# Inverting the delta rule's triangular matrices on 64x64 blocks, two products side by side in the array

## The chip, the cores and the metric

The kernel runs on one core of one Trainium2 chip. The metric is the device time of one execution in microseconds (us). Several engines work beside each other on their own instruction queues: TensorE (PE; its weight loads are listed apart as PEld), VectorE (DVE), ScalarE (ACT), GpSimd (POOL) and SyncE (SP), which issues most transfers. They meet through semaphores.

## The reference

The reference is a two-layer hybrid block (attention, state-space scan, stick-breaking attention, feed-forward nets), followed by a second block. In the second block a gated delta net (8 heads of width 64, 256 tokens) stands beside a window attention, and a mixture of experts comes after it. All inputs are float32. What matters here is the delta rule, which the reference computes in chunks of 64 tokens:

```
m = jnp.where(strict, jnp.einsum('bhncd,bhnsd->bhncs', kb, k) * decay, 0.0)
eye = jnp.eye(CHUNK, dtype=jnp.float32)
a_mat = eye + m
t_mat = lax.linalg.triangular_solve(a_mat, jnp.broadcast_to(eye, a_mat.shape),
                                    left_side=True, lower=True)
u = jnp.einsum('bhncs,bhnse->bhnce', t_mat, vb)
w = jnp.einsum('bhncs,bhnsd->bhncd', t_mat, kb * jnp.exp(G)[..., None])
attn = jnp.einsum('bhncd,bhnsd->bhncs', q, k) * decay
```

The output of a delta rule does not depend on the length of the chunks; the kernel takes chunks of 128 tokens, so that it has two chunks (t = 0, 1) of 8 heads: 16 triangular matrices of 128x128 to invert.

## The kernel before, in words

Nearly all of the kernel is matrix products with weights that stream through a ring of buffers; each is split in a rounded part and a rest (`round_chunk` L247 on ACT, `split_chunk` L251 on DVE) and multiplied in three passes (`three`, L264 to L266). The change is in one class, `DeltaRule`, which runs once, between the input projection of the second block (`Project`) and `WindowAttention`. During it SP and POOL have nothing to do; the next weights already lie in the ring.

Heads are handled in two groups, e = 0 and e = 1 (even and odd heads); a group has 8 matrices, s = 4t + h. Three engines work in an order written out by hand, and every engine takes its instructions in program order:

- `pe_spread` (L2195) writes the cumulated decay of each head along a row, `dve` subtracts the column's own (L2401), ACT takes the exponential (L2312), and DVE multiplies by the causal mask (L2406). `pe_gram` (L2203) makes k^T kb and k^T q with 64 rows of the array for each product: e = 0 lies in rows 0 to 63, e = 1 in rows 64 to 127. DVE multiplies them with the decays to `mT` (L2409) and `aT` (L2414).
- Then the inverse T of I + M grows by doubling. At level v the inverses of the diagonal blocks of size 2^v are known, and `LmT` holds the part of M that couples neighbouring blocks (`mT` times the mask of the level, L2411 and L2421). PE makes L T (`l_times_t`, L2220), ACT and DVE copy it out of PSUM (L2318 and L2418), PE makes T L T and its transpose (`update`, L2227 and L2228), and DVE subtracts both (L2436 and L2437) and masks the next `LmT`. There are 7 levels for 128 rows: the first needs no update product, the last only one; levels 2 to 6 run in a hardware loop (`Fori`). Each product is 128x128x128 and takes two records of PE. Both T and its transpose `Tt` are kept, since a product needs its stationary operand transposed.
- The tail (L2252 to L2274) uses `Tt` for the values of the first chunk, the state, and the second chunk; ACT brings the output to `br` (L2325), and DVE normalises it (L2462).

Of the kernel before, what the change touches and what calls it, by code (L numbers as in the profile page):

```python
# [34 lines left out]
P = 128  # L35
# [31 lines left out]
LEVELS = 7  # L67
# [20 lines left out]
def shape_constants():  # L88
# [11 lines left out]
    ]  # L100
    for b in [1 << n for n in range(LEVELS)]:
        parts.append((f"level{b}", ((j // b) % 2 == 1) & (p // b == j // b - 1)))
# [29 lines left out]
def build(nc, A, out, stop=99):  # L132
# [1957 lines left out]
    class DeltaRule:  # L2090
# [13 lines left out]
        SPREAD_BANK, KK_BANK, QK_BANK, FIRST_BANK = (0, 6), (2, 4), (0, 6), (2, 4)  # L2104
        level, lt, upd = sem("g_level"), sem("g_lt"), sem("g_upd")
        lt0_done, lt1_done = sem("g_lt0_done"), sem("g_lt1_done")
        u0, u0_done, wT_done, state, state_done = (sem(f"g_{n}") for n in ("u0", "u0_done", "wT_done", "state", "state_done"))
        vnew, vnew_done, out_done = sem("g_vnew"), sem("g_vnew_done"), sem("g_out")
# [11 lines left out]
        LT = e  # L2120
        LmT = [view(room, 12288 + 1024 * e, 8, P) for e in range(2)]
        T = [merged[:, e, :].rearrange("p (s n) -> p s n", n=P) for e in range(2)]
        Tt = [view(xT_work, D * e, 8, P) for e in range(2)]
        vn = [view(hi_ring, 3072 + 512 * e, 8, HD2) for e in range(2)]
# [25 lines left out]
        def pool(self, pool):  # L2150
# [8 lines left out]
            self.multiply(nc.gpsimd, self.kd, self.k_, self.tab[:, 5, 0, :], 0).then_inc(self.scaled2, 1)  # L2159
            pool.wait_ge(pow_asked, power(2))  # L2160
# [45 lines left out]
        def pe(self, pe):  # L2206
# [7 lines left out]
            heads = self.heads  # L2214
            carry(pe)

            def l_times_t(e, stat, bank=None):
                for t, h in heads:
                    s = 4 * t + h
                    ins = pe.matmul(ps[:, (4 * e if bank is None else bank) + t, h * P:(h + 1) * P], self.LmT[e][:, s, :], stat(s), start=True, stop=True)  # L2220
                ins.then_inc(self.lt, 1)

            def update(e, both):
                for t, h in heads:
                    s, cols = 4 * t + h, slice(h * P, (h + 1) * P)
                    if both:
                        pe.matmul(ps[:, 4 * e + 2 + t, cols], self.Tt[e][:, s, :], self.LT[e][:, s, :], start=True, stop=True)  # L2227
                    ins = pe.matmul(ps[:, 4 * e + t, cols], self.LT[e][:, s, :], self.Tt[e][:, s, :], start=True, stop=True)  # L2228
                ins.then_inc(self.upd, 1)
            for e in range(2):  # L2230
                pe.wait_ge(self.level, e + 1)
                l_times_t(e, lambda s: ident, self.FIRST_BANK[e])
            with pe.Fori(0, LEVELS - 2) as v:
                for e in range(2):
                    pe.wait_ge(self.level, v * 2 + (e + 3))
                    l_times_t(e, lambda s: self.T[e][:, s, :])
                for e in range(2):
                    pe.wait_ge(self.lt0_done, v * 2 + (e + 1))
                    pe.wait_ge(self.lt1_done, v * 2 + (e + 1))
                    update(e, True)  # L2240
            for e in range(2):
                pe.wait_ge(self.level, LEVELS * 2 + e - 1)
                l_times_t(e, lambda s: self.T[e][:, s, :])
            for e in range(2):
                pe.wait_ge(self.lt0_done, LEVELS * 2 + e - 3)
                pe.wait_ge(self.lt1_done, LEVELS * 2 + e - 3)
                update(e, False)
            cols = lambda h: slice(h * HD2, (h + 1) * HD2)
            for e in range(2):
                pe.wait_ge(self.level, LEVELS * 2 + e + 1)  # L2250
# [3 lines left out]
                ins.then_inc(self.u0, 1)  # L2254
            for e in range(2):
                pe.wait_ge(self.u0_done, e + 1)
                for h in range(4):
                    ins = pe.matmul(ps[:, 4 * e + 2, cols(h)], self.both(self.kd, 0, h), self.vn[e][:, h, :], start=True, stop=True)
                ins.then_inc(self.state, 1)
            for e in range(2):  # L2260
                pe.wait_ge(self.wT_done, e + 1)
                pe.wait_ge(self.state_done, e + 1)
# [4 lines left out]
                ins.then_inc(self.vnew, 1)  # L2267
            for e in range(2):
                pe.wait_ge(self.vnew_done, e + 1)
# [5 lines left out]
                ins.then_inc(self.out_done, 1)  # L2275
# [29 lines left out]
        def act(self, act):  # L2305
# [9 lines left out]
            with act.Fori(0, LEVELS - 1) as v:  # L2315
                for e in range(2):
                    act.wait_ge(self.lt, v * 2 + (e + 3))
                    nc.scalar.copy(self.LT[e][:, 0:4, :], view_bank(4 * e, 4, P)).then_inc(self.lt0_done, 1)  # L2318
            for e in range(2):
                act.wait_ge(self.u0, e + 1)  # L2320
                nc.scalar.copy(self.rows(self.wT, e), self.rows(view_bank(4 * e + 1, 4, P), e)).then_inc(self.wT_done, 1)
            for e in range(2):
                act.wait_ge(self.out_done, e + 1)
# [63 lines left out]
        def dve(self, dve):  # L2387
# [7 lines left out]
            lev = consts[:, CONSTS["level1"][0]:CONSTS["level1"][0] + LEVELS * P].rearrange("p (v n) -> p v n", n=P)  # L2395
            dve.wait_ge(self.scaled2, 1)
            for e in range(2):
                dve.wait_ge(self.gram, (self.SPREAD0, self.SPREAD1)[e])
                for s in range(8):
                    t, h = divmod(s, 4)  # L2400
                    ins = V.tensor_scalar(self.e[e][:, s, :], ps[:, self.SPREAD_BANK[e] + t, h * P:(h + 1) * P], self.tab[:, 1, t, 2 * h + e:2 * h + e + 1],  # L2401
                                          0.0, ALU.subtract, ALU.min)
                ins.then_inc(self.seg, 1)
            for e in range(2):
                dve.wait_ge(self.dec, e + 1)
                V.tensor_tensor(self.e[e], self.e[e], bc(const("upto").unsqueeze(1), [P, 8, P]), ALU.mult)  # L2406
                dve.drain()
                dve.wait_ge(self.gram, self.KK)
                V.tensor_tensor(self.mT[e], self.e[e], big(self.KK_BANK[e]), ALU.mult)  # L2409
                dve.drain()  # L2410
                V.tensor_tensor(self.LmT[e], self.mT[e], bc(lev[:, 0:1, :], [P, 8, P]), ALU.mult).then_inc(self.level, 1)  # L2411
            dve.wait_ge(self.gram, self.QK)
            for e in range(2):
                V.tensor_tensor(self.aT[e], self.e[e], big(self.QK_BANK[e]), ALU.mult)  # L2414
            eye = bc(ident.unsqueeze(1), [P, 8, P])

            def copy_lt(e):
                V.tensor_copy(self.LT[e][:, 4:8, :], view_bank(4 * e + 1, 4, P)).then_inc(self.lt1_done, 1)  # L2418

            def next_level(e, mask):  # L2420
                V.tensor_tensor(self.LmT[e], self.mT[e], bc(mask, [P, 8, P]), ALU.mult)  # L2421
                dve.drain()
                dve.sem_inc(self.level, 1)
            for e in range(2):
                dve.wait_ge(self.lt, e + 1)
# [1011 lines left out]
```

## Time and profile before

| | |
|---|---|
| Median of 3 runs | 2549.4 us (2544.87 to 2549.5) |
| Profiled execution | 2549.39 us, of which the span 2547.5 us |
| PE busy | 2315.7 us, 91% of the span |
| DVE busy | 1683.0 us, 66% |
| ACT busy | 1157.6 us, 45% |
| Mean granted clock of TensorE | 0.939 of full speed |
| Delta rule, from the end of L2401 to the first product of the tail | 1938.74 to 2027.75 us of the span |
| Its tail | 2027.75 to 2062 us |

"Busy" is the share of time in which the engine has an instruction under way. The granted clock is 1.0 at 2.4 GHz and 0.5 at 1.2 GHz. Line numbers (L2220) are those of the kernel before.

### The profile page before, as it was taken

How to read it: one execution, taken by the hardware profiler on the slowest of the kernel's cores; microseconds unless marked ns; L12 is line 12 of the kernel's file. 1: busy time of each engine (PE TensorE's matmuls, PEld its weight loads, DVE VectorE, ACT ScalarE, POOL GpSimd, SP SyncE). 2: the span in 40 equal slices, each digit the busy share in tenths (PEclk: the TensorE clock that was granted, in tenths of full speed). 3: DMA queues.
4: the chain of work that ended last, by engine and by line, in shares of the span. 5: the costliest groups of instructions: out<-in, count | busy, mean ns of one | idle time of the engine just before them, and what ended most of it. 6: DMA issues, size and time to landing. Idle time of an engine off the chain costs nothing.

```text
span 2547.5 us, 32468 instructions
## 1 busy us (share of the span) xinstructions
PE 2315.7 (91%) x11904; PEld 1958.9 (77%) x11904; DVE 1683.0 (66%) x2158; ACT 1157.6 (45%) x1664; POOL 354.2 (14%) x141
## 2 busy tenths in 40 slices
PE   8998998899989989989989899899797847999999
PEld 6887887778868878878887688688687836887877
DVE  5765665478667757756654687677566643667997
ACT  4444453364444434444533644444352013546875
POOL 3531000000025315410000000244001010000000
PEclk9998999889989989999988899899899956999999
DMA  8765543234657657656432345576340000657996
GB/s 299 237 211 150 166 133 104 88 124 136 195 184 237 214 164 237 226 153 175 132 109 86 113 145 181 174 238 225 108 140 10 0 1 6 208 189 252 358 361 235
DMA packets 320162, 426.91 MB, mean 168 GB/s; under 512 B 28192, under 2 KB 220080, under 8 KB 319904
## 3 DMA queue, kind: packets, MB, share of 16 engines
q1 hardware_dynamic: 315904, 412.45, 50.7%
q0 software_dynamic: 4016, 12.73, 1.7%
q8 instruction: 77, 1.26, 0.2%
q14 instruction: 53, 0.43, 0.1%
q10 hardware_dynamic: 112, 0.04, 0.0%
HBM read 424.06 MB, written 1.05 MB: 167 GB/s over the span
## 4 chain that ended last, share of the span: by engine, by line
PE 74%; DVE 8%; issue 8%; ACT 6%; DVEq 2%; DMA 1%; POOL 1%; PEld 1%; POOLq 0%; SPq 0%; ACTq 0%; PEldq 0%
PE ps L264 17%; PE ps L266 17%; PE ps L265 17%; PE ps L511 10%; PE ps L3167 4%; ACT hi L247 3%; DVE lo L251 2%; PE ps L297 2%; PE ps L1053 1%; ACT room L929 1%; DVE room L1138 1%; PE ps L502 1%; DMA raw<-in_w_up 1%; DVEq L1095 1%; DVEq L730 1%
## 5 line engine op out<-in xcount | busy, mean ns | idle before, releaser
L251 DVE TENSOR_TENSOR lo<-raw,hi 128x1024 fp32r<-128x1024 f32 x737 | 1012.6, 1389 | 618.3 <-ACT hi L247 612.2
L247 ACT CAST hi<-raw 128x1024 fp32r<-128x1024 f32 x737 | 769.1, 1048 | 867.9 <-PE ps L266 695.9
L264 PE MATMUL ps<-hi,xT_hi 128*128 128x512 f32 (+2 forms) x1440 | 575.9, 400 | 5.7 <-issue 5.0
L266 PE MATMUL ps<-hi,xT_lo 128*128 128x512 f32 (+2 forms) x1440 | 563.2, 391 | 0.0
L265 PE MATMUL ps<-lo,xT_hi 128*128 128x512 f32 (+2 forms) x1440 | 563.1, 391 | 0.0
L264 PEld LDWEIGHTS ps<-hi,xT_hi 128*128 128x128 f32 x1440 | 280.5, 195 | 58.7 <-issue 6.5
L266 PEld LDWEIGHTS ps<-hi,xT_lo 128*128 128x128 f32 x1440 | 279.7, 194 | 57.2
L265 PEld LDWEIGHTS ps<-lo,xT_hi 128*128 128x128 f32 x1440 | 280.6, 195 | 51.4
L681 POOL TENSOR_SCALAR room<-room,vecs 128x1536 f32<-128x1536 f32 x28 | 134.9, 4819 | 235.8 <-DMA room<-in_w_ada 235.8
L264 PE MATMUL ps<-xT_hi,hi 128*128 128x256 f32 x544 | 160.9, 296 | 0.0
L265 PE MATMUL ps<-xT_lo,hi 128*128 128x256 f32 x544 | 155.4, 286 | 0.0
L266 PE MATMUL ps<-xT_hi,lo 128*128 128x256 f32 x544 | 155.3, 285 | 0.0
L511 PE MATMUL ps<-hi,hidT_hi 128*128 128x512 f32 x352 | 138.8, 394 | 9.2 <-DVE hidT_lo L597 9.2
L511 PE MATMUL ps<-lo,hidT_hi 128*128 128x512 f32 x352 | 138.3, 393 | 0.0
L511 PE MATMUL ps<-hi,hidT_lo 128*128 128x512 f32 x352 | 138.2, 393 | 0.0
L264 PEld LDWEIGHTS ps<-xT_hi,hi 128*128 128x128 f32 x544 | 106.0, 195 | 4.5 <-issue 4.0
L265 PEld LDWEIGHTS ps<-xT_lo,hi 128*128 128x128 f32 x544 | 106.0, 195 | 0.1
L266 PEld LDWEIGHTS ps<-xT_hi,lo 128*128 128x128 f32 x544 | 105.7, 194 | 0.0
L683 POOL TENSOR_TENSOR room<-room 128x1536 f32<-128x1536 f32 x28 | 103.0, 3679 | 8.1 <-issue 4.7
L264 PE MATMUL ps<-hi,brT_hi 128*128 128x512 f32 x224 | 91.5, 408 | 3.9 <-DVE lo L251 3.9
L265 PE MATMUL ps<-lo,brT_hi 128*128 128x512 f32 x224 | 90.2, 403 | 0.0
L266 PE MATMUL ps<-hi,brT_lo 128*128 128x512 f32 x224 | 90.0, 402 | 0.0
(526 smaller groups left out, 3348.6 us busy)
## 6 DMA issues: line engine op xcount, KB each, us to landing
raw<-in_w_mix_in SPq DMA_DIRECT2D x368, 256.0 KB, 2.9
raw<-in_ffn_w_in SPq DMA_DIRECT2D x352, 256.0 KB, 3.4
raw<-in_ffn_w_out SPq DMA_DIRECT2D x176, 256.0 KB, 2.9
raw<-in_w_gate SPq DMA_DIRECT2D x128, 256.0 KB, 5.1
raw<-in_w_up SPq DMA_DIRECT2D x128, 256.0 KB, 6.6
raw<-in_w_down SPq DMA_DIRECT2D x128, 256.0 KB, 5.7
room<-in_w_ada SPq DMA_DIRECT2D x32, 768.0 KB, 6.4
raw<-in_w_branch SPq DMA_DIRECT2D x96, 256.0 KB, 3.0
```

Source lines behind the costliest of these rows:

```text
L247: nc.scalar.copy(hi[c.hi_slot][:, 0:c.cols], raw[c.slot][:, 0:c.cols]).then_inc(rounded, 1)
L251: nc.vector.tensor_tensor(lo[c.slot][:, 0:c.cols], raw[c.slot][:, 0:c.cols], hi[c.hi_slot][:, 0:c.cols], ALU.subtract).then_inc(split, 1)
L264: pe.matmul(out, a[0], b[0], start=start, stop=False)
L265: pe.matmul(out, a[0], b[1], start=False, stop=False)
L266: return pe.matmul(out, a[1], b[0], start=False, stop=stop)
L297: ins = pe.transpose(ps[:, bank, at:at + P], self.src[:, t, k * P:(k + 1) * P], ident)
L502: ins = pe.transpose(ps[:, 6 + t, k * P:(k + 1) * P], hid[:, t, k * P:(k + 1) * P], ident)
L511: ins = pe.matmul(ps[:, 2 * t + half, :], a[p], w[q][:, cols], start=first and n == 0, stop=False, skip_group_check=True)
L681: nc.gpsimd.tensor_scalar(self.rows(k), self.rows(k), cols2[:, k:k + 1], None, ALU.mult)
L683: nc.gpsimd.tensor_tensor(pieces.acc, pieces.acc, self.rows(k), ALU.add).then_inc(pieces.multiplied, 1)
L730: dve.drain()
L3167: ins = pe.matmul(ps[:, self.sums(tile) + half, :], a[p], w[q][:, cols], start=first and n == 0, stop=False, skip_group_check=True)
```

## The change

The inverse is computed for the two diagonal 64x64 blocks of each 128x128 matrix by themselves, and a last step couples them.

- `T`, `T_t` and `U` hold the two 64x64 blocks of a matrix one above the other: rows 0 to 63 and rows 64 to 127 of 64 columns, 8 matrices in 512 columns. Six levels remain (`LEVELS` 7 to 6).
- Every product of the levels is two products of 64x64x64, one with the operands in rows 0 to 63 and the result in partitions 0 to 63, one with all of it in 64 to 127.
- The mask of the level is put on the product and no more on M: `U` = mask times (M^T T), one instruction of DVE that also brings it out of PSUM. `LmT`, the copies on ACT and DVE and the `drain` ahead of each level's signal go.
- Level 0 uses a stacked identity in place of T; its product for T is left out, its product for the transpose waits for `aT`, which now comes after the level's masks (its banks are needed again).
- The last step multiplies the coupling block of M with the lower block's inverse and the upper's: 8 products of 64x64x64 per group, twice; ACT copies the diagonal blocks into `Tt` and writes the third block with the sign turned; POOL has cleared the fourth.
- The causal mask is added as a large negative number ahead of the exponential (`scalar_tensor_tensor` in place of `tensor_scalar`), so that L2406 goes.
- The hardware loops are written out; the semaphores of the tail are merged into two.

```diff
-LEVELS = 7
+LEVELS = 6
+        ("upto_least", np.where(p <= j, 0, NEG)),
...
-        parts.append((f"level{b}", ((j // b) % 2 == 1) & (p // b == j // b - 1)))
+        parts.append((f"level{b}", (p % half // b == c // b + 1) & (c // b % 2 == 0)))
+    parts.append(("eye_half", p % half == c))
...
+        U_BANK, T_BANK, TT_BANK = (2, 4), (3, 5), (0, 6)
...
+            pool.wait_ge(self.split, self.SPLIT_QG)
+            for e in range(2):
+                ins = nc.gpsimd.memset(self.Tt[e][:, :, 0:HD2], 0.0)
+            ins.then_inc(self.cleared, 1)
...
+            for v in range(LEVELS):
+                for e in range(2):
+                    if v == 0:
+                        pe.wait_ge(self.mats, self.MT + e + 1)
+                    else:
+                        pe.wait_ge(self.level, 2 * (v - 1) + e + 1)
+                    for s in range(8):
+                        for r in self.halves:
+                            ins = pe.matmul(ps[r, self.U_BANK[e], slot(s)], self.mT[e][r, s, r], self.T[e][r, slot(s)] if v else eye[r], start=True, stop=True)
+                    ins.then_inc(self.lt, 1)
+                for e in range(2):
+                    pe.wait_ge(self.masked, 2 * v + e + 1)
+                    if v:
+                        pe.wait_ge(self.level_t, 2 * (v - 1) + e + 1)
+                        for s in range(8):
+                            for r in self.halves:
+                                ins = pe.matmul(ps[r, self.T_BANK[e], slot(s)], self.T_t[e][r, slot(s)], self.U[e][r, slot(s)], start=True, stop=True)
+                        ins.then_inc(self.upd, 1)
+                    else:
+                        pe.wait_ge(self.mats, self.AT + e + 1)
+                    for s in range(8):
+                        for r in self.halves:
+                            ins = pe.matmul(ps[r, self.TT_BANK[e], slot(s)], self.U[e][r, slot(s)], self.T_t[e][r, slot(s)] if v else eye[r], start=True, stop=True)
+                    ins.then_inc(self.upd_t, 1)
...
-            with act.Fori(0, LEVELS - 1) as v:
-                for e in range(2):
-                    act.wait_ge(self.lt, v * 2 + (e + 3))
-                    nc.scalar.copy(self.LT[e][:, 0:4, :], view_bank(4 * e, 4, P)).then_inc(self.lt0_done, 1)
+            for e in range(2):
+                act.wait_ge(self.level_t, 2 * (LEVELS - 1) + e + 1)
+                for r in self.halves:
+                    nc.scalar.copy(self.Tt[e][r, :, r], slots(self.T_t[e][r]))
+            for e in range(2):
+                act.wait_ge(self.upd_t, 2 * LEVELS + e + 1)
+                nc.scalar.mul(self.Tt[e][low, :, high], slots(ps[low, self.TT_BANK[e], :]), -1.0).then_inc(self.inverse, 1)
...
+            for v in range(LEVELS):
+                mask = bc(const(f"level{1 << v}").unsqueeze(1), [P, 8, HD2])
+                for e in range(2):
+                    dve.wait_ge(self.lt, 2 * v + e + 1)
+                    V.tensor_tensor(slots(self.U[e]), slots(ps[:, self.U_BANK[e], :]), mask, ALU.mult).then_inc(self.masked, 1)
+                    if v == 0:
+                        dve.drain()
+                        V.tensor_tensor(slots(self.T[e]), eye, slots(self.U[e]), ALU.subtract).then_inc(self.level, 1)
...
+                for e in range(2):
+                    if v:
+                        dve.wait_ge(self.upd, 2 * (v - 1) + e + 1)
+                        V.tensor_tensor(self.T[e], self.T[e], ps[:, self.T_BANK[e], :], ALU.subtract).then_inc(self.level, 1)
+                    dve.wait_ge(self.upd_t, 2 * v + e + 1)
+                    V.tensor_tensor(slots(self.T_t[e]), slots(self.T_t[e]) if v else eye, slots(ps[:, self.TT_BANK[e], :]), ALU.subtract).then_inc(self.level_t, 1)
+                dve.drain()
```

## Rows read from the trace of the kernel before

**Rows 1.** Chain that ended last, 1900 to 2110 us: start, length, what.
```profile
1920.99 138.09 issue
```

**Rows 2.** Stretches: length, busy us (instructions) of each engine, clock, DMA share, GB/s.
```profile
1938.74:2027.75 89.01, 72.77 (x608) 70.00 (x609) 60.87 (x57) 12.03 (x17) 0.00 (x0) 0.96 0.00 0
2027.75:2062.00 34.25, 27.73 (x130) 23.86 (x128) 7.06 (x12) 2.45 (x6) 2.88 (x1) 0.60 0.00 0
...
1952.93:1959.75 6.82, 6.12 (x29) 5.82 (x29) 3.53 (x5) 0.65 (x2) 0.00 (x0) 0.50 0.01 2
1959.75:2034.80 75.05, 66.68 (x569) 64.39 (x569) 47.23 (x49) 7.55 (x13) 0.00 (x0) 1.00 0.00 0
2034.80:2086.00 51.20, 24.34 (x90) 20.27 (x91) 19.49 (x35) 2.31 (x5) 6.43 (x2) 0.50 0.00 0
```

**Rows 3.** Timeline of PE: start, busy us, what, records, idle before.
```profile
1938.79 2.06 PE L2203 MATMUL ps<-hi_ring 64*128 64x128 f32 x32 [1.60 <-DVE room L2401]
...
1952.10 3.07 PE L2220 MATMUL ps<-merged,room 128*128 128x128 f32 x16 [3.80 <-DVEq L2422]
1955.87 3.78 PE L2220 MATMUL ps<-merged,room 128*128 128x128 f32 x16 [0.70 <-DVEq L2422]
...
1966.93 2.05 PE L2220 MATMUL ps<-merged,room 128*128 128x128 f32 x16
1970.62 2.05 PE L2220 MATMUL ps<-merged,room 128*128 128x128 f32 x16 [1.63 <-DVEq L2422]
...
2018.61 2.05 PE L2220 MATMUL ps<-merged,room 128*128 128x128 f32 x16
...
2031.33 1.90 PE L2258 MATMUL ps<-hi_ring,room 128*128 128x64 f32 x16
2033.26 0.41 PE L2265 MATMUL ps<-room,xT_work 128*128 128x64 f32 x2
2033.59 0.43 PE L2266 MATMUL ps<-hi_ring,room 64*128 64x64 f32 x2
2033.95 0.43 PE L2265 MATMUL ps<-room,xT_work 128*128 128x64 f32 x2
```

**Rows 4.** Timeline of DVE around the first level.
```profile
1934.52 4.22 DVE L2401 TENSOR_SCALAR room<-ps,small 128x128 f32<-128x128 f32 x16
...
1946.11 2.34 DVE L2414 TENSOR_TENSOR room<-room,ps 128x1024 f32<-128x1024 f32 x2
```

**Rows 5.** Groups by line, 1900 to 2062 us: count, busy us, mean ns, idle before.
```profile
L2421 DVE TENSOR_TENSOR room<-room,consts 128x1024 f32<-128x1024 f32 x12 | 14.6, 1219 | 0.1
L2436 DVE TENSOR_TENSOR merged<-merged,ps 128x1024 f32<-128x1024 f32 x10 | 12.2, 1221 | 15.5 <-PE ps L2228 15.5
...
L2145 DVE TENSOR_TENSOR room<-room,small 128x512 f32<-128x512 f32 x7 | 6.2, 930 | 0.2
L2401 DVE TENSOR_SCALAR room<-ps,small 128x128 f32<-128x128 f32 x16 | 4.2, 340 | 0.0
...
L2321 ACT COPY room<-ps 64x512 f32<-64x512 f32 x2 | 1.2, 580 | 6.0 <-PE ps L2253 6.0
```

**Rows 6.** Groups of DVE over the whole span, two shapes that the change needs.
```profile
L833 DVE TENSOR_TENSOR room<-room,ps 128x512 f32<-128x512 f32 x16 | 10.2, 680 | 0.0
...
L1017 DVE SCALAR_TENSOR_TENSOR hidden<-hidden,room,vecs 128x128 f32<-128x128 f32 x32 | 8.6, 344 | 0.0
```

**Rows 7.** Single instructions by line: ns least/median/most, first and last start.
```profile
L2203 PE MATMUL ps<-hi_ring x64: 272/272/373, 1935.1 to 1940.6; 64*128 64x128 f32 x64
...
L2228 PEld LDWEIGHTS ps<-xT_work,room x192: 192/192/232, 1959.7 to 2027.5; 128*128 128x128 f32 x192
...
L2630 PEld LDWEIGHTS ps<-consts,hi_ring x16: 131/177/177, 2082.3 to 2085.8; 128*64 128x64 f32 x16
```

**Rows 8.** Stretches around the window attention's first products, columns as in rows 2.
```profile
2082.30:2086.00 3.70, 3.63 (x18) 3.05 (x19) 0.42 (x1) 1.02 (x1) 0.00 (x0) 0.50 0.02 4
2086.00:2090.00 4.00, 3.40 (x22) 2.93 (x21) 0.42 (x2) 2.30 (x2) 0.00 (x0) 1.00 0.00 0
```

More of the change, by code:

```diff
@@ L2103, in build @@
         SPREAD0, SPREAD1, KK, QK = 1, 2, 3, 4
[L2104 to L2108, printed above, removed]
+        SPREAD_BANK, KK_BANK, QK_BANK = (0, 6), (2, 4), (0, 6)
+        level, level_t, upd, upd_t = sem("g_level"), sem("g_level_t"), sem("g_upd"), sem("g_upd_t")
+        mats, lt, masked, cleared, inverse = sem("g_mats"), sem("g_lt"), sem("g_masked"), sem("g_cleared"), sem("g_inverse")
+        MT, AT = 0, 2
+        U_BANK, T_BANK, TT_BANK = (2, 4), (3, 5), (0, 6)
+        tail, tail_done, wT_done = sem("g_tail"), sem("g_tail_done"), sem("g_wT_done")
+        U0, STATE, VNEW, OUT = 1, 3, 5, 7
         raw = room[0:CT * CONV, 14000:14000 + P]
@@ L2119, in build @@
         e, mT, aT = ([view(room, 6144 + 2048 * n + 1024 * e, 8, P) for e in range(2)] for n in range(3))
-        LT = e
-        LmT = [view(room, 12288 + 1024 * e, 8, P) for e in range(2)]
-        T = [merged[:, e, :].rearrange("p (s n) -> p s n", n=P) for e in range(2)]
+        U = [room[:, 12288 + 512 * e:12288 + 512 * (e + 1)] for e in range(2)]
+        T = [merged[:, 0, 512 * e:512 * (e + 1)] for e in range(2)]
+        T_t = [merged[:, 1, 512 * e:512 * (e + 1)] for e in range(2)]
         Tt = [view(xT_work, D * e, 8, P) for e in range(2)]
+        halves = [slice(0, HD2), slice(HD2, P)]
         vn = [view(hi_ring, 3072 + 512 * e, 8, HD2) for e in range(2)]
@@ L2213, in pe @@
             self.pe_gram(pe, self.QK_BANK, self.qT)
[L2214 to L2220, printed above, removed]
-                ins.then_inc(self.lt, 1)
[L2223 to L2229, printed above, removed]
@@ L2241, in pe @@
[L2241 to L2247, printed above, removed]
+            slot = lambda s: slice(s * HD2, (s + 1) * HD2)
+            eye = const("eye_half")
+            for v in range(LEVELS):
[22 more added lines that the diff above has]
+                    ins.then_inc(self.upd_t, 1)
@@ new lines, in pe @@
+            low, high = self.halves
+            for e in range(2):
+                pe.wait_ge(self.level, 2 * (LEVELS - 1) + e + 1)
+                for s in range(8):
+                    ins = pe.matmul(ps[high, self.U_BANK[e], slot(s)], self.mT[e][low, s, high], self.T[e][low, slot(s)], start=True, stop=True)
+                ins.then_inc(self.lt, 1)
+            for e in range(2):
+                pe.wait_ge(self.masked, 2 * LEVELS + e + 1)
+                pe.wait_ge(self.level_t, 2 * (LEVELS - 1) + e + 1)
+                for s in range(8):
+                    ins = pe.matmul(ps[low, self.TT_BANK[e], slot(s)], self.U[e][high, slot(s)], self.T_t[e][high, slot(s)], start=True, stop=True)
+                ins.then_inc(self.upd_t, 1)
@@ L2403, in dve @@
                 ins.then_inc(self.seg, 1)
+            dve.wait_ge(self.gram, self.KK)
             for e in range(2):
                 dve.wait_ge(self.dec, e + 1)
-                V.tensor_tensor(self.e[e], self.e[e], bc(const("upto").unsqueeze(1), [P, 8, P]), ALU.mult)
-                dve.drain()
[L2408 to L2411, printed above, removed]
@@ L2412, in dve @@
-            dve.wait_ge(self.gram, self.QK)
-            for e in range(2):
[L2414 to L2423, printed above, removed]
```

84 lines of the change are left out of this document (32 added, 52 removed).

## The prediction

> **What bounds the kernel now.** I read the table of stretches first, then the chain of waits, and since the chain is blind here, the timelines of PE and DVE. Between 1920.99 and 2059 us the chain shows only "issue", 138.09 us long [rows 1]: it came along an engine that waited for one signal all the while, and says nothing of the delta rule. The stretches do. From the end of L2401 (1934.52 + 4.22 = 1938.74) to the tail (2027.75) 89.0 us pass, in which PE is busy for 72.8, DVE for 60.9 and ACT for 12.0, at a mean clock of 0.96, and no transfer runs [rows 2]. So nothing outside this chain of three engines hides the stretch: what it loses, the kernel loses, and what it gains has no transfer to run into.
>
> Inside, one level repeats: L2220 starts at 1966.93, and for the fourth time after it at 2018.61, so a level takes 12.92 us [rows 3]. It has 48 products of 128x128x128. Of the 12.92 PE idles 1.63 ahead of the second group's L2220 [rows 3] and some 0.2 ahead of the first's; the rest, 11.1 us, is 0.23 per product. DVE waits for PE once per level for most of the 15.5 us that L2436 waited in all [rows 5]. So PE sets the pace of a level.
>
> **The change, part by part.** Its own time of the profiled execution is 2549.39 us, the same as the median of the runs, so one number serves for both.
>
> *Price of a pair.* In the new levels the unit is a pair: two 64x64x64 products, one in rows 0 to 63, one in rows 64 to 127, four records. A level has 6 groups of 8 pairs, 48 pairs. The nearest row is the gram product (L2203), which also pairs the two halves of the rows: 32 records, hence 16 products, in 2.06 us [rows 3], of which 0.27 is the length of the last record [rows 7]. That is (2.06 - 0.27)/31 = 58 ns per record, 0.23 us per pair with 128 weight columns and 128 moving columns, half of what L2220 needs per product (16 records in 2.05 us): the halves do run side by side. The new pair halves both column counts. If the time goes with them, it costs 0.115: the lower end, since L2220's 128 columns take that long per record and 64 cannot take under half of it with two records in turn in each half. That weight loads do shrink is in the trace: the shortest with 64 columns is 131 ns long, the usual one with 128 columns 192 [rows 7]. The upper end is 0.23: no record denser than the 58 ns of the gram. I take 0.135, near the lower end, because the load and the stream, the two things that 58 ns was made of, both halve, with some added for instructions that now must come twice as densely as anywhere in the trace.
>
> The Trainium skill ("TensorE: Matmul & The Clock Gate", "Back-to-back issue gap") has a rule against this: with hardware decode off the sequencer spends about 62 ns on every matmul, however small. By it a pair would cost 0.25, a level 12, and the kernel would come out near 2543. The gram's 58 ns per record is below that, so the slow mode does not seem to be on, and what chance it has is counted with the first rival; the same section's other floor, about 25 ns between starts, gives 0.10 per pair and binds nothing.
>
> *A level.* 48 x 0.135 = 6.5 us of PE. Its waits: the first group's update needs the masked product, 0.27 after its last record, plus 0.68 for one 128x512 instruction of DVE [rows 6] and 0.15 for two signals, 1.1 us; the other group's 8 pairs cover 1.08 of it. The other waits are covered by 16 pairs or more. DVE has 6 instructions of 0.6 to 0.68, 4.1 us, and ACT nothing: neither binds. So 6.6 us per level instead of 12.92; five such levels (1 to 5) make 33.0.
>
> *Level 0.* From 1938.7 the QK gram holds PE to 1940.7, as before. L2406 is gone (two of 1.2 us), and so are both first masks (L2411); `mT` of the first group is ready at 1939.9, hidden behind the gram. Group U0 ends at 1941.8, U1 at 1942.9. DVE: mask and T for both groups until 1944.8, then `aT` (2.34, L2414 [rows 4]) until 1947.1; the transposes' products follow at 1946.0 and 1947.2 and end at 1948.3. Sum: 9.6 us up to level 1. The `scalar_tensor_tensor` for 128x128 costs 344 ns against the 340 of `tensor_scalar` [rows 5, 6]: nothing.
>
> *Clock, first place.* In that order PE idles some 3.1 us (1942.9 to 1946.0). Before, an idle of 3.80 us at 1952.10 was followed by 6.82 us at 1.2 GHz, in which 16 records took 3.78 us instead of 2.05 [rows 2, 3]; that cost 3.4 us, half the stretch. It is part of the 89.0. The new idle is a little shorter: between 0 and 3.4, I take 2.5.
>
> *The coupling.* One group after the other, 16 records in a single tile: 0.9 us at 58 ns each, 0.35 for result and signal, 0.69 for DVE, 0.1, again 0.9 and 0.35, and 0.68 for ACT (0.58 for 64x512, L2321 [rows 5], and a signal): 4.0 us. The second group trails by 0.9 and lies under the tail's products of the first. ACT's four copies into `Tt` (4 x 0.58) lie under PE's and DVE's half of it; without that cover they would cost 2.3.
>
> *Sum of the stretch*: 9.6 + 2.5 + 33.0 + 4.0 = 49.1 instead of 89.0: 39.9 less.
>
> *Clock, second place.* The tail starts at 2.4 GHz and falls to 1.2 at 2034.8 [rows 2], 7.0 us in, after records of only 64 columns behind weight loads of 128 (L2258 and after [rows 3]). The coupling ahead of it now has idle gaps, so it may fall earlier, for up to 7.0 us more: I take 3.0.
>
> *POOL.* Two memsets of 512 columns fall beside DVE's copies at about 1931. DVE instructions of 128x512 beside POOL took 930 ns instead of 680 (L2145 against L833 [rows 5, 6]); two such meetings, 0.5. The bound is 0 to 2. What it clears is awaited 50 us later.
>
> *Written-out loops, merged semaphores, smaller constants*: the profile shows no idle at loop ends beyond the signals, so nothing; instruction fetch is in the upper end of the pair's price.
>
> In all 39.9 - 3.0 - 0.5 = 36.4 us less: 2549.4 - 36.4 = **2513**.
>
> **The rivals.** Write p for the price of a pair; up to level 1 the stretch takes 6.4 + 24p, then 240p + 0.5, and the rest above.
>
> *Records no denser than before* (the two tiles in turn, or the queue feeding one record per 58 ns; in effect the change does not do what it says). p = 0.23: level 0 takes 11.9, five levels 55.7, clock 2.5, coupling 5. Sum 75.1, 13.9 less, minus 3.5: 2539. At p = 0.18 it is 2525. For it: nothing in the trace is denser. Against it: the gram's 58 ns is just what 128 columns need.
>
> *The slow clock all through.* A product in two corners of the array leaves half of it idle, and PE may count as little used. p = 0.23 to 0.27, level 0 12, levels 56 to 65, coupling 5.8 (records twice as long), the tail 7.0 longer: 2542 to 2552. For it: the fall in the tail. Against: L2630 and L2632 fill 64 columns only, and after 3.63 busy of 3.70 us of them the clock went from 0.50 to 1.00 [rows 8]; PE will be busy almost without a gap in the levels.
>
> *Slower: every change of tile has a price.* L2265 and L2266 alternate between 128 and 64 rows of the array: 0.33 to 0.36 us apart at full clock [rows 3] where L2258, of one shape, needs 1.90/8 = 0.24; a change costs 0.11. If the change between the two halves, after every product of the levels, costs that too, a pair costs 0.115 x 2 + 0.22 = 0.45. Then level 0 takes 17, the levels 108.5, with 2.5 and 4.0: 132, 43 more than before, and 3.5: 2596. It turns slower from 264p + 13.4 = 85.5 on, p = 0.27. Against it: the gram changes halves after each product and shows none of it. The Trainium skill ("TensorEngine Tiling", "Key Properties") says that a change of the tiling mode drains the array, but not one of the tile within it. By that rule the drain comes at the stage's two edges only; no row has 64x64 tiles.
>
> **How the numbers follow.** What this kernel's measurement can tell from no change is about 0.2%, 5.1 us. Forecast (p from 0.115 to 0.17, hence 2505 to 2524, with the clock terms at their other ends): 0.58. Records no denser (2524 to 2541): 0.20. Slow clock (2538 to 2553): 0.13, of which 0.05 within 0.2%. Price of the change of tile (2552 to 2600): 0.09. Faster: 0.58 + 0.20 + 0.07 = 0.85, with 0.01 of the slow clock for slower: same 0.05, slower 0.10. The range of 8 in 10 runs from 2504 over the forecast and most of the second case to 2541.
>
> **What would show it right or wrong.** The levels' first products should start 6.6 us apart (5.7 to 8.3); at 11 the records are no denser, at 22 the tile changes cost. The four records of a pair should lie in some 135 ns. The clock should be 1.00 in levels 2 to 5. DVE should be busy for about 4 us of each level. From the end of L2401's successor to the tail there should be 49 us. It would be wrong if p is not what halves, or if a wait between the engines is longer than the 1.1 us I gave it: then PE idles in every level.

## Result and the profile after

| | before | after |
|---|---|---|
| Median | 2548.14 us of 4 runs (2544.87 to 2549.5) | 2502.22 us of 4 runs (2500.06 to 2506.0) |
| Profiled execution, its span | 2549.39, 2547.5 | 2500.21, 2498.1 |
| Delta rule up to its tail, from the QK gram product on | 89.0 us | 42.8 us |
| From there to the window attention's first products | 54.6 | 53.6 |
| From there to the router | 80.9 | 75.9 |
| From the router to the end | 384.2 | 388.4 |

The ratio is 0.9822 [0.9808, 0.9835]: 46 us less, beyond the lower end of the range (2504) and 10.8 us under the forecast of 2513. The direction and the pace of the levels by PE came as forecast; the price of a pair and the clock in the tail did not.

The busy line of the page after, and stretches of its trace with the columns of [rows 2]: the stage from the QK gram to the tail, from there to the window attention, the slow clock in level 0, the levels under the full clock with the tail's start, and one level.

```profile
PE 2279.3 (91%) x12480; PEld 1925.2 (77%) x12480; DVE 1660.5 (66%) x2142; ACT 1152.8 (46%) x1658; POOL 356.2 (14%) x143
...
1937.35:1980.19 42.84, 39.59 (x1185) 39.26 (x1185) 30.67 (x42) 8.03 (x10) 0.00 (x0) 0.96 0.01 3
1980.19:2033.78 53.59, 26.71 (x131) 23.11 (x130) 21.45 (x40) 3.04 (x7) 6.43 (x2) 0.58 0.00 0
1944.70:1948.10 3.40, 3.40 (x66) 3.40 (x68) 1.64 (x2) 0.00 (x0) 0.00 (x0) 0.52 0.02 5
1948.10:1989.10 41.00, 40.97 (x1097) 40.13 (x1092) 25.43 (x40) 4.80 (x8) 0.00 (x0) 1.00 0.01 4
1953.74:1959.42 5.68, 5.68 (x199) 5.68 (x197) 4.14 (x6) 0.00 (x0) 0.00 (x0) 1.00 0.03 6
```

The last line answers to the 12.92 us of [rows 3]. PE has work in every moment of a level, DVE 4.14 us of 5.68, ACT none, and the clock is 1.00. The stage as a whole has PE busy for 39.59 of 42.84 us, where it was 72.8 of 89.0 [rows 2]. On the whole page PE's busy time fell by 36 us and its share stayed at 91%.

The timeline of PE (start, length, what, records, idle before) shows level 0, level 1, level 2, and the way into the tail. Line numbers are the changed kernel's: L2213 is the gram product, L2234 the product for U, L2242 and L2248 the ones for T and its transpose, L2254 and L2260 the coupling, L2266 the tail's first.

```profile
1937.35 2.06 PE L2213 MATMUL ps<-hi_ring 64*128 64x128 f32 x32 [1.60 <-DVE room L2420]
1939.34 2.08 PE L2234 MATMUL ps<-consts,room 64*64 64x64 f32 x64
1944.67 3.57 PE L2248 MATMUL ps<-consts,room 64*64 64x64 f32 x64 [3.25 <-DVE room L2440]
1948.06 2.05 PE L2234 MATMUL ps<-merged,room 64*64 64x64 f32 x64
...
1953.74 2.03 PE L2234 MATMUL ps<-merged,room 64*64 64x64 f32 x64
1955.63 1.15 PE L2242 MATMUL ps<-room,merged 64*64 64x64 f32 x32
1956.62 1.10 PE L2248 MATMUL ps<-merged,room 64*64 64x64 f32 x32
1957.55 1.10 PE L2242 MATMUL ps<-room,merged 64*64 64x64 f32 x32
...
1976.44 1.85 PE L2254 MATMUL ps<-merged,room 64*64 64x64 f32 x29
1978.18 2.08 PE L2260 MATMUL ps<-merged,room 64*64 64x64 f32 x32
1980.19 0.44 PE L2266 MATMUL ps<-room,xT_work 128*128 128x64 f32 x2
```

Read the starts: 8 pairs of L2242 take 1956.62 - 1955.63 = 0.99 us, the 8 of L2248 after them 0.93, and so on. A pair costs 0.93/8 = 0.117 us, one record 0.029. In the coupling, where all records of a group lie in one tile, 32 of them need 2.0 us, 0.06 each. And in level 0 the 64 records of L2248, after 3.25 us of idle, take 3.4 us where 16 pairs at 0.117 take 1.9: that is the slow clock of 1944.7 to 1948.1, 1.5 us of it. Between the levels and the tail PE has no gap: its 64 records of the coupling take the 4.0 us from 1976.2 to 1980.19.

The timeline of DVE in one level:

```profile
1956.83 0.69 DVE L2444 TENSOR_TENSOR merged<-merged,ps 128x512 f32<-128x512 f32 x1 [0.32 <-PE ps L2242]
1957.76 0.69 DVE L2446 TENSOR_TENSOR merged<-merged,ps 128x512 f32<-128x512 f32 x1 [0.25 <-PE ps L2248]
...
1959.63 0.69 DVE L2446 TENSOR_TENSOR merged<-merged,ps 128x512 f32<-128x512 f32 x1 [0.25 <-PE ps L2248]
1960.56 0.69 DVE L2433 TENSOR_TENSOR room<-ps,consts 128x512 f32<-128x512 f32 x1 [0.25 <-PE ps L2234]
```

Every instruction of DVE waits for PE, for 0.25 us or a little more, and PE waits for none of them. Six of them fit a level as six groups of pairs do: 0.69 + 0.25 = 0.94 against 0.93.

### The profile page after: what moved, and what is told of

Its sections match the earlier page's. It is cut to its first block, busy times and chain, and to the rows that moved or that the text cites. A ratio compares the mean times of both kernels' runs of the same rounds, so it can differ in the third digit from the quotient of the medians.

```text
span 2498.1 us, 33499 instructions
## 1 busy us (share of the span) xinstructions
PE 2279.3 (91%) x12480; PEld 1925.2 (77%) x12480; DVE 1660.5 (66%) x2142; ACT 1152.8 (46%) x1658; POOL 356.2 (14%) x143
## 4 chain that ended last, share of the span: by engine, by line
PE 77%; DVE 7%; ACT 6%; issue 5%; DVEq 2%; DMA 1%; PEld 1%; POOL 1%; POOLq 0%; ACTq 0%; PEldq 0%; SPq 0%
PE ps L267 18%; PE ps L269 18%; PE ps L268 18%; PE ps L514 10%; PE ps L3171 4%; ACT hi L250 3%; DVE lo L254 2%; PE ps L300 2%; PE ps L1056 1%; ACT room L932 1%; DVE room L1141 1%; PE ps L505 1%; DMA raw<-in_w_up 1%; DVEq L1098 1%; DVEq L733 1%
## 5 line engine op out<-in xcount | busy, mean ns | idle before, releaser
L686 POOL TENSOR_TENSOR room<-room 128x1536 f32<-128x1536 f32 x28 | 109.0, 3894 | 8.1 <-issue 4.7
```

The source lines that it names most:

```text
L686: nc.gpsimd.tensor_tensor(pieces.acc, pieces.acc, self.rows(k), ALU.add).then_inc(pieces.multiplied, 1)
```

## Experiments

The theory (A): the levels go at PE's pace, a pair costs what 64 moving columns and loads of 64 columns cost because two tiles work at once, and what is left of slow clock lies in level 0 and the tail. Its rivals: (B) the chain through DVE is as tight as PE; (C) the gain is that of the masks and copies that went, not that of the small products; (D) single small products would do as well, without pairing. Each stage below is "from the QK gram to the tail".

**The changed kernel once more** (again), no edit.

> The changed kernel as it is, beside the kernel before, to have its time in the same rounds as the three edits next to it. Expected 2502 us, within 3 us, and again 5.68 us per level in levels 1 to 5 with the clock at 1.00. If the 46 us gain were partly luck of where the slow stretches of TensorE's clock fall, the time would lie at 2507 or more and the spans of the runs would differ.

2501.35 us of 5 runs (2499.26 to 2502.62), ratio 0.9811 [0.9797, 0.9825]; the stage 42.8, and from the router to the end 389.6. A second profile of before, taken later, has 89.0, 54.6, 80.9 and 384.0 for the stages of the table above. The result and its stages repeat.

**Records one tile after the other** (turns). The two loops of every group change places: eight products in rows 0 to 63, then eight in 64 to 127.

```diff
-                    for s in range(8):
-                        for r in self.halves:
+                    for r in self.halves:
+                        for s in range(8):
```

> The changed kernel with the order of the products turned: in each group first the 8 products of rows 0 to 63, then the 8 of rows 64 to 127; same products, same results. Theory (a pair costs 0.117 us because neighbours in the queue lie in different halves of the array and run at once): without alternation a pair costs 0.23, a level 11.2 us instead of 5.7, and the kernel takes 27 to 30 us more than the changed one, about 2530. Rival (two records cost 0.058 each by themselves, whatever lies beside them, because of the halved columns alone): 5.7 us per level and no change.

2568.0 us of 4 runs (2564.84 to 2570.34), ratio 1.0076 [1.0058, 1.0094]: slower than before. The stage took 100.6 us. Stretches of it (the first products; 99 us of the stage and its tail; one level), and the first products in PE's timeline:

```profile
1943.60:1947.00 3.40, 3.40 (x66) 3.27 (x64) 1.68 (x3) 3.00 (x4) 0.00 (x0) 1.00 0.00 0
1948.90:2047.90 99.00, 98.11 (x1115) 98.02 (x1116) 25.74 (x37) 4.22 (x7) 0.00 (x0) 0.50 0.01 1
1955.50:1971.58 16.08, 16.08 (x197) 16.08 (x195) 4.13 (x6) 0.00 (x0) 0.00 (x0) 0.50 0.01 2
```
```profile
1943.60 3.40 PE L2234 MATMUL ps<-consts,room 64*64 64x64 f32 x64
1949.80 5.64 PE L2248 MATMUL ps<-consts,room 64*64 64x64 f32 x61 [2.79 <-DVE room L2440]
```

Two things come apart here. At the full clock (1943.60) 64 records take 3.40 instead of 2.08 us, 0.050 each instead of 0.029: that is what working side by side is worth. And the clock stayed at 0.50 for 99 us, although PE was busy for 98.11 of them. It fell at 1948.9, in the 2.79 us of idle ahead of L2248, as it fell at the end of the changed kernel's gap; there it was back at 1.00 after 3.4 us of products, here it did not come back. No run has this order without the gap, so whether the clock would have stayed at 1.00 then is open. A level of 192 records takes 16.08 us; at 0.050 per record it would take 9.6. So of the 10.4 us by which a level is longer than the changed kernel's 5.68, 3.9 are lost pairing and 6.5 lost clock. Theory D falls. The expectation (about 2530) named only the first; the kernel took 38 us more than that.

**Whole weights** (wide). One product of 128x128 weights and 64 moving columns in place of each pair. For the time only: the stationary operand is the whole `mT` in every product, so the inverse isn't computed.

```diff
-                        for r in self.halves:
-                            ins = pe.matmul(ps[r, self.U_BANK[e], slot(s)], self.mT[e][r, s, r], self.T[e][r, slot(s)] if v else eye[r], start=True, stop=True)
+                        ins = pe.matmul(ps[:, self.U_BANK[e], slot(s)], self.mT[e][:, s, :], self.T[e][:, slot(s)] if v else eye, start=True, stop=True)
```

> The changed kernel with one product of 128 rows and 128 weight columns by 64 moving columns in place of each pair (the weights are always M's 128x128, so the results of the levels are not the reference's). It has half as many records. Theory (the pair's price is set by the longer of load and stream, and both had to be halved): the load of 128 columns sets 0.235 us per product, twice the pair's price though each record streams the same 64 columns; a level takes 11.3 us, and the kernel 28 us more than the changed one, 2530, or up to 30 us more still if the clock falls. Rival (the moving columns alone set the price): 0.115 per product, no change.

2590.59 us of 4 runs (2585.42 to 2593.09), ratio 1.0164 [1.0144, 1.0185]; the stage 124.6. Stretches (122.9 us of it; one level) and the first product at the full clock:

```profile
1946.20:2069.10 122.90, 121.68 (x603) 121.47 (x604) 26.06 (x37) 4.22 (x7) 0.00 (x0) 0.50 0.00 1
1954.28:1974.76 20.48, 20.48 (x98) 20.48 (x98) 4.13 (x6) 0.00 (x0) 0.00 (x0) 0.50 0.00 0
```
```profile
1940.84 3.79 PE L2233 MATMUL ps<-consts,room 128*128 128x64 f32 x32
```

A product of 64 moving columns behind a load of 128 costs 3.79/16 = 0.24 us at the full clock, what L2258 needed before [rows 3], and about twice the pair's 0.117. Per record that is 0.118; in the coupling a record with a load of 64 columns, 64 rows and the same 64 moving columns takes 0.06. So the smaller load (with the smaller tile) halves a record, and two tiles at once halve it again. Fewer moving columns alone gain nothing: a record of L2220, with 128 of both, took 0.12 too [rows 3]. Again the clock falls in the gap of level 0 (2.79 us) and stays down, though PE is busy for 121.68 of 122.90 us. That cost more than the 30 us that the expectation allowed for it: 2590.6 where at most 2560 was expected.

**Only the masks' part of the change** (masks). The kernel before, with the mask put on the product in DVE's copy and no more on M; 128x128 products as before.

```diff
-                    nc.scalar.copy(self.LT[e][:, 0:4, :], view_bank(4 * e, 4, P)).then_inc(self.lt0_done, 1)
...
-                V.tensor_copy(self.LT[e][:, 4:8, :], view_bank(4 * e + 1, 4, P)).then_inc(self.lt1_done, 1)
+                V.tensor_tensor(self.LT[e], big(4 * e), bc(mask, [P, 8, P]), ALU.mult).then_inc(self.lt1_done, 1)
...
-                V.tensor_tensor(self.LmT[e], self.mT[e], bc(mask, [P, 8, P]), ALU.mult)
```

> One part alone, on the kernel before: the level's mask is put on the product, in the one instruction of DVE that brings it out of PSUM; no LmT after the first level and no copies on ACT and DVE. The products stay 128x128x128 and the levels 7. Theory: this part closes PE's idle of 1.8 us per level, so levels take 10.9 to 11.3 us instead of 12.9: 9 to 12 us less than the kernel before, about 2538, and the other 34 to 37 us of the change are the halved products. Rival (DVE binds, with three instructions of 128x1024 for each group and level, 7.3 us, in a chain with PE): no gain or a loss.

2543.81 us of 10 runs (2538.66 to 2547.68), ratio 0.998 [0.997, 0.9989]; the stage 78.4. The first level with updates and a later one as stretches, and PE's timeline:

```profile
1952.00:1963.51 11.51, 11.09 (x97) 10.90 (x98) 7.16 (x6) 0.00 (x0) 0.00 (x0) 1.00 0.01 1
1975.21:1986.91 11.70, 11.01 (x98) 10.82 (x97) 7.15 (x6) 0.00 (x0) 0.00 (x0) 1.00 0.00 0
```
```profile
1952.00 2.05 PE L2221 MATMUL ps<-merged,room 128*128 128x128 f32 x16 [2.50 <-DVEq L2416]
1954.47 2.05 PE L2221 MATMUL ps<-merged,room 128*128 128x128 f32 x16 [0.42 <-DVEq L2416]
...
1977.85 2.05 PE L2221 MATMUL ps<-merged,room 128*128 128x128 f32 x16 [0.69 <-DVEq L2416]
```

10.6 us less in the stage. Level 1 took 11.5 instead of 14.8 us (1952.10 to 1966.93 in [rows 3]), and the slow stretch of [rows 2] did not come: 3.3. The four levels after it took 11.7 each instead of 12.92: 4.9. The rest, 2.3, lies in level 0 and the last level. The levels are longer than the expected 10.9 to 11.3, since PE still idles 0.69 in each. So 10.6 of the 46.1 us come with the masks alone, and 35.5 only with the small products; theory C holds for less than a quarter. The whole kernel gained 5.8 only, where 9 to 12 were expected; where 4 us of the rest went is told with the tail below.

**DVE slower by one instruction** (slow_mask2). Ahead of each mask from level 1 on, the same 128x512 instruction into a table that is no longer needed.

```diff
                     dve.wait_ge(self.lt, 2 * v + e + 1)
+                    if v:
+                        V.tensor_tensor(self.e[e][:, :, 0:HD2], slots(ps[:, self.U_BANK[e], :]), mask, ALU.mult)
```

> The changed kernel with one more instruction of 128x512 ahead of each mask in levels 1 to 5, on DVE, whose result nobody reads (two per level, 1.2 us more of DVE's 4.1). Theory A (PE alone binds, DVE has 1.5 us per level to spare): no change, 5.68 us per level. Theory B (the wait for the first group's masked product is already as long as the other group's products that cover it): each level takes 0.6 us longer, 6.3 us, and the stretch of the delta rule 3 us.

2506.55 us of 4 runs (2503.8 to 2506.86), ratio 0.9828 [0.9813, 0.9843]; the stage 45.8. PE's timeline around one level (the last row is cut off by the window):

```profile
1955.94 2.03 PE L2234 MATMUL ps<-merged,room 64*64 64x64 f32 x64
1958.43 1.15 PE L2242 MATMUL ps<-room,merged 64*64 64x64 f32 x32 [0.46 <-DVE room L2435]
...
1962.21 0.98 PE L2234 MATMUL ps<-merged,room 64*64 64x64 f32 x28
```

A level takes 6.27 us, 0.6 more, for 0.69 us added ahead of the product that waits for the mask. Theory B holds as well as A: PE never waits in the changed kernel, but it has hardly any slack: 0.6 of the 0.69 us arrives, 0.46 of it as idle ahead of L2242. The prediction's 1.1 us of wait covered by 1.08 us of pairs was this balance. By this a faster PE alone should gain little; no run tried one.

**Level 0 without its gap** (early). The transpose's product of level 0 goes to the T banks, which are free then, and waits no more for `aT`; the half of `aT` for e = 0 comes ahead of the masks, the other half after those of level 1.

```diff
-                    else:
+                    if v == 1:
                         pe.wait_ge(self.mats, self.AT + e + 1)
...
-                            ins = pe.matmul(ps[r, self.TT_BANK[e], slot(s)], ...
+                            ins = pe.matmul(ps[r, (self.TT_BANK if v else self.T_BANK)[e], slot(s)], ...
...
```

> Level 0 of the changed kernel: its product for the transpose goes to the banks of T, which are free at that level, and so waits no more for aT; the first group's aT comes ahead of the first mask, the second group's after the masks of level 1. Theory (PE's idle of 3.25 us in level 0 is on the path, and the 3.4 us at 1.2 GHz after it are its consequence): level 1 starts about 4 us sooner, PE idles less than 1.5 us at a time, and no stretch at 1.2 GHz is left before the tail; 4 to 5.5 us less than the changed kernel. Rival (DVE's order only moves the same wait to level 1, since aT has to be made anyway): less than 1 us gained, with an idle of PE of 1 to 2 us in level 1.

2498.26 us of 5 runs (2492.56 to 2504.01), ratio 0.9803 [0.9783, 0.9822]. The whole stage as a stretch, and level 0:

```profile
1937.71:1976.31 38.60, 38.35 (x1185) 37.87 (x1185) 30.14 (x42) 8.03 (x10) 0.00 (x0) 1.00 0.01 4
```
```profile
1941.79 1.15 PE L2248 MATMUL ps<-consts,room 64*64 64x64 f32 x32
1943.17 1.15 PE L2248 MATMUL ps<-consts,room 64*64 64x64 f32 x32 [0.23 <-DVE room L2435]
1944.15 2.03 PE L2234 MATMUL ps<-merged,room 64*64 64x64 f32 x64
```

The gap of 3.25 us is now 0.23, the clock 1.00 all through, and the stage 4.2 us shorter: the gap itself and the slow clock that followed it. In the medians it is 3.1 us against "again", within the spread of the runs.

**The gap filled with work** (filler): 48 products without use, 96 records, between the two products of level 0.

```diff
+                if v == 0:
+                    for n in range(3):
+                        for s in range(8):
+                            for r in self.halves:
+                                pe.matmul(ps[r, self.T_BANK[1], slot(s)], self.mT[1][r, s, r], eye[r], start=True, stop=True)
```

> The changed kernel with 48 more products of 64x64x64 (2.8 us of PE) in PE's idle of 3.25 us in level 0, whose results nobody reads. Theory (the 3.4 us at 1.2 GHz that follow this idle are caused by it): the slow stretch is gone, the 64 records of the level's second half take 2.1 us instead of 3.57, and the kernel is 1 to 2 us faster for doing more work. Rival (the slow stretch has another cause, or the fillers delay the product behind them by as much): no change, or up to 1 us slower.

2505.45 us of 4 runs (2503.96 to 2506.26), ratio 0.9833 [0.9816, 0.9851]. PE's timeline:

```profile
1943.11 2.97 PE L2240 MATMUL ps<-consts,room 64*64 64x64 f32 x96
1946.53 2.28 PE L2253 MATMUL ps<-consts,room 64*64 64x64 f32 x64 [0.45 <-DVE room L2445]
```

The records after it started as late after the gram as before (7.32 us) but took 2.28 instead of 3.57 us, at a clock of 1.00, and the stage 41.6 instead of 42.8: the fall followed the gap. Yet the kernel as a whole was not 1 to 2 us faster, as expected, but 3 to 4 us slower in the medians. In the profiles the stretch from window attention to router took 81.8 us instead of 75.9.

**The tail by shapes** (tail). The tail alternates between products with 128 and with 64 rows. Here they go in groups of four of one shape. For the time only: in this form the start flag stands on every first product of a sum while others in its PSUM bank are open, and the sums come out incomplete. The run both3 below, in which only the flags differ from both, gives them whole.

```diff
                 for h in range(4):
-                    o = ps[:, 4 * e + 3, cols(h)]
-                    pe.matmul(o, self.Tt[e][:, 4 + h, :], self.head(self.vb, 1, e, h), start=True, stop=False)
-                    ins = pe.matmul(o, self.rows(self.wT, e)[:, h, :], ...
+                    pe.matmul(ps[:, 4 * e + 3, cols(h)], self.Tt[e][:, 4 + h, :], self.head(self.vb, 1, e, h), start=True, stop=False, ...
+                for h in range(4):
+                    ins = pe.matmul(ps[:, 4 * e + 3, cols(h)], self.rows(self.wT, e)[:, h, :], ...
...
```

> The tail of the changed kernel with its products grouped by the rows they use: in each group all products over 128 rows first, then all over 64 rows; same count, same results. Theory (a change between 128 and 64 rows costs about 0.1 us at 2.4 GHz and 0.2 at 1.2): 6 us less, products about 0.43 us apart at 1.2 GHz instead of 0.62. Rival (no price for the change; the product over 64 rows is slow by itself): within 1 us of the changed kernel, and the products over 64 rows stay 0.6 us apart.

2501.29 us of 5 runs (2492.84 to 2503.18), ratio 0.9803 [0.9785, 0.9821]. First the tail in the changed kernel, then in this one:

```profile
1992.15 0.69 PE L2279 MATMUL ps<-room,xT_work 128*128 128x64 f32 x2
1992.77 0.69 PE L2280 MATMUL ps<-hi_ring,room 64*128 64x64 f32 x2
1993.39 0.69 PE L2285 MATMUL ps<-hi_ring,room 128*128 128x64 f32 x2
1994.00 0.69 PE L2287 MATMUL ps<-hi_ring,room 64*128 64x64 f32 x2
1994.62 0.69 PE L2288 MATMUL ps<-hi_ring,room 128*128 128x64 f32 x2
1995.10 0.64 PE L2285 MATMUL ps<-hi_ring,room 128*128 128x64 f32 x2
```
```profile
1987.52 1.08 PE L2278 MATMUL ps<-room,xT_work 128*128 128x64 f32 x8
1988.53 1.10 PE L2280 MATMUL ps<-hi_ring,room 64*128 64x64 f32 x8
...
1996.06 1.97 PE L2288 MATMUL ps<-hi_ring,room 64*128 64x64 f32 x8
```

In turn a product costs 0.62 us at the half clock; four of one shape 1.9, 0.47 each. At the full clock it is 0.25 in groups (1987.52 to 1988.53) against 0.33 to 0.36 in turn [rows 3]. The changed kernel shows it by itself: from L2288 to L2285, without a change of rows, 0.48 us pass, where a change costs 0.62. It is not the sum into one output that costs: L2280 adds to the output of the L2279 ahead of it, and the next L2279 starts another, yet both steps take 0.62. The tail up to the window attention took 48.5 us instead of 53.6. The Trainium skill ("TensorEngine Tiling", "Key Properties") says that a change of the tiling mode drains the array, but not a change of the tile within it. The trace agrees as far as prices go: the first costs 0.11 to 0.15 us per change in the tail, the second nothing that shows in the levels, whose pairs change tile after every product.

Here too the kernel as a whole kept none of it. The stretch from window attention to router, first in the repeated run of the changed kernel, then in this one:

```profile
2034.10:2110.00 75.90, 51.44 (x252) 43.81 (x253) 32.48 (x50) 29.20 (x63) 1.37 (x2) 0.79 0.02 5
```
```profile
2030.40:2111.90 81.50, 57.51 (x252) 49.41 (x253) 32.76 (x50) 29.49 (x63) 1.36 (x2) 0.69 0.02 5
```

The same 252 records, with a clock of 0.79 or of 0.69: 5.6 us. In all profiles this stretch takes 75.9 to 77.3 us or 80.9 to 81.8, whichever kernel it is: both profiles of before have 80.9. No edit here touched it; by the clocks it depends on where its sparse products meet the slow clock, but what decides that is not shown. From the router to the end both profiles of before take 384, slow_mask2 385.6 and the others 388 to 390, masks too (388.4), whose products are still the large ones. The clock is 0.98 there in both profiles of before and 0.97 in those of the changed kernel and of masks, which is about the size of the 4 us; why it differs is open.

**Both together** (both), and with the start flag on a bank's first product alone, so that the sums are whole (both3).

```diff
...
-                    pe.matmul(ps[:, 4 * e, cols(h)], self.aT[e][:, h, :], self.vn[e][:, h, :], start=True, stop=True)
-                    pe.matmul(ps[:, 4 * e, cols(4 + h)], self.aT[e][:, 4 + h, :], ..., start=True, stop=False, ...
+                    pe.matmul(ps[:, 4 * e, cols(h)], self.aT[e][:, h, :], self.vn[e][:, h, :], start=(h == 0), stop=False, ...
+                    pe.matmul(ps[:, 4 * e, cols(4 + h)], self.aT[e][:, 4 + h, :], ..., start=False, stop=False, ...
```

> Both edits: level 0 without the wait for aT, and the tail grouped by rows. If both theories hold the gains add up: 10 to 11 us less than the changed kernel, some 2492 us. If the clock falls earlier in the tail, because it no longer had a slow stretch ahead of the levels, up to 3 us of that are lost.

> Level 0 without the wait for aT and the tail grouped by rows, with the start flag set only on the first product of each PSUM bank in the grouped tail, so that the results are the reference's. Same instructions and order as the run named both, so the same times: 38.6 us from the QK gram to the tail, 47.7 us from there to the window attention, 2490 us in all. If the flag had a price or the earlier results had changed the pace, the tail would be off by more than 0.5 us.

both: 2489.69 us (2485.89 to 2491.83), ratio 0.9766 [0.9751, 0.9781]. both3: 2491.22 us (2488.68 to 2492.1), 0.9772 [0.9759, 0.9786], each of 5 runs. The two edits by themselves had medians 3.1 and 0.1 us under "again", together they are 11.7 under it. Most of the 8.5 us between lies in the stretch from window attention to router: 77.3 us in early and 81.5 in tail, but 76.0 in both. The stages of both3, up to the tail and up to the window attention:

```profile
1936.15:1974.65 38.50, 38.26 (x1184) 37.82 (x1184) 30.09 (x42) 8.02 (x10) 0.00 (x0) 1.00 0.02 4
1974.65:2022.35 47.70, 20.85 (x131) 19.83 (x128) 21.45 (x40) 3.04 (x7) 6.43 (x2) 0.60 0.00 1
```

It is the version that beats both kernels, by 10 to 11 us below the changed one (the ranges of the runs don't touch) and 58 below the kernel before.

## Why the prediction was right and where it failed

| step | forecast | measured |
|---|---|---|
| price of a pair | 0.135 (0.115 to 0.23) | 0.117 |
| a level | 6.6 | 5.68 |
| level 0 and its slow clock | 9.6 + 2.5 | 10.7, of which about 1.5 clock |
| five levels | 33.0 | 28.2 |
| coupling | 4.0 | 4.0 |
| stage up to the tail | 49.1 | 42.8 |
| tail's clock | +3.0 | -1.0 |
| POOL | +0.5 | no cost seen |
| start of the stage | as before | 1.4 earlier, within the spread of the profiles |
| the rest of the kernel | 0 | -5.0 and +4.2 |

*What held.* The stage that nothing hides, PE as what sets a level's pace, the idle in level 0 (3.1 forecast, 3.25 measured) with a slow stretch behind it, and DVE's 4.1 us per level came as worked out. The coupling's 4.0 us came too, but by another way: it was forecast as one group's chain through PE, DVE and ACT, and is PE alone, which has to make both groups' 64 records of some 0.06 us ahead of the tail. Of the rivals, "records no denser" was refuted by 0.029 us per record, half of the 58 ns. With that the 62 ns per matmul that the Trainium skill ("TensorE: Matmul & The Clock Gate", "Back-to-back issue gap") gives for hardware decode switched off does not apply here either. "Every change of tile has a price" was refuted in the levels and is real in the tail.

*The price of a pair* is the first step that failed. The two bounds were the gram's 0.23 and half of it, 0.115, and the value taken lay a little above the lower "for instructions that must come twice as densely". No such cost shows: 0.117. Over 264 pairs that is 4.8 of the 6.3 us by which the stage was overestimated; the other 1.5 are mostly the slow clock of level 0, taken at 2.5 and worth 1.5. That term was read too high in the trace of before: of the 3.4 us only 1.9 reached the end of the level, which took 14.83 us (1952.10 to 1966.93) against 12.92, in part because PE idled 0.70 ahead of the second group and not 1.63 [rows 3].

*The clock, second place* is the other. The tail was to fall to the half clock earlier because of idle gaps in the coupling. There were none: PE was busy for 40.97 of the 41.00 us from level 1 to the fall, the second group's products lying in the first's waits. The clock fell 8.9 us after the tail's first product (1989.1 against 1980.2), not 7.1 as before [rows 2]; why later is not shown. In all, the stage after the levels was 1.0 us shorter, not 3.0 longer.

*POOL's* 0.5 rested on a mean: L2145's 930 ns [rows 5] mix instructions of 679 ns, the median, with some of up to 1577. The start that came 1.4 us earlier says nothing of POOL: the stage starts between 1935.2 and 1941.6 in the profiles, at 1937.4 and 1937.7 in the changed kernel's two and at 1939.2 in filler, which is the same up to there.

*The sum of the misses*: 6.3 (stage), 4.0 (tail's clock), 1.9 (POOL's 0.5 and the earlier start) and 0.8 (the two later stretches) are 13.0 us, and 2513 - 13.0 = 2500, the profiled execution. It has to come out, since the stages make up the span; 2.2 us of it (start and later stretches) belong to no step of the forecast. *The range* failed by its own working: with p at 0.115 and both clock terms at zero the sum is 2513 - 5.3 - 2.5 - 3.0 = 2502, while the text gave 2505 for these ends. That 2502 is also the median is luck: the slow clock of level 0 cost 1.5 and not zero, and the tail gained 1.0. And it had no term for what the stages downstream do when they start at another time, 5 us either way in the runs above.

*The rival that was underrated* is the slow clock all through. It did not come, but not because PE is busy without a gap, as the prediction argued: in turns and wide PE was just as busy and the clock stayed at 0.50 for 99 and 123 us. Turns differs from the changed kernel in the order of the tiles alone. So it is their alternation that brought the overlap and, after the gap of level 0, the full clock back. With the loops the other way round the same change would have cost 18 us.

## What to carry to other kernels

Products of 64x64 paid here because neighbours in the queue alternate between two tiles of the array: a pair then cost half of a 128x128 product (0.117 against 0.23 us), and the full clock held. Where both counts of columns halve, take the half as the forecast and a supplement only as the bound, and sum all bounds at once for the range. Before adding a cost for idle gaps, look whether another group's products fill them. When an edit's local gain doesn't reach the end, read the clock of the later sparse stages in both profiles before doubting the edit.

## What was not expected of the hardware

- PE busy for 98.11 of 99.00 us at a granted clock of 0.50 (turns), and 121.68 of 122.90 (wide): being busy in the record did not bring the full clock back.
- Two tiles in alternation need 0.029 us per record, one tile at a time 0.050 (turns) to 0.06 (the coupling), all with 64 moving columns at the full clock.
- A change between 128 and 64 rows cost 0.11 us at the full clock and some 0.15 at the half, and grouping by shape took 5.1 us from the tail.
- One and the same stage took 75.9 or 81.5 us, by where its slow stretches fell (mean clock 0.79 or 0.69).
